# A decoder layer on one core: scaling, casts, sums and weights in a new order between w_o and the second SwiGLU, and in the first pair of both SwiGLUs

## The reference, cut to what matters

```
x = x + 1/2 * gate1(c) * SwiGLU_1(adaLN_1(RMSNorm(x), c))
h = adaLN_2(RMSNorm(x), c)
y = W_o( sigmoid(g_nsa(h)) * Up_nsa(NSA(h)) + sigmoid(g_fox(h)) * Up_fox(FoX(h)) )
x = x + gate2(c) * y
x = x + 1/2 * gate3(c) * SwiGLU_2(adaLN_3(RMSNorm(x), c))
out = RMSNorm(x)

rms_norm(x, g)  = x * rsqrt(mean(x * x) + eps) * g
swiglu(h)       = (silu(h @ w_gate) * (h @ w_up)) @ w_down        # 1024 -> 2816 -> 1024
```

## Time and profile before

| | us |
|---|---|
| median of 3 runs | 2421.49 |
| lowest and highest | 2418.65, 2422.41 |
| the profiled execution, device time | 2420.48 |
| its span, first to last instruction | 2418.8 |
| mean granted TensorE clock in it | 0.985 |

### The profile page before, as it was taken

How to read it: one execution, slowest core, us unless ns; L and a number is a source line. 1 busy time by engine, 2 the same in 40 slices (tenths; PEclk the granted TensorE clock), 3 DMA queues, 4 the chain that set the end, 5 groups by cost and what they waited for, 6 DMA issues and landing times. The chain is left out here.

```text
span 2418.8 us, 30082 instructions
## 1 busy us (share of the span) xinstructions
PE 2310.0 (96%) x10920; PEld 1881.7 (78%) x10920; DVE 1394.3 (58%) x1667; ACT 1087.5 (45%) x2060; POOL 1251.1 (52%) x964
## 2 busy tenths in 40 slices
PE   4999999999999899999999999999989999999997
PEld 2788888888878777778777877787768888888885
DVE  5845565356556755653688888568663323325544
ACT  3533333333444543334788888424533333323332
POOL 3454444444664555445557555456645555535463
PEclk7999999999999999999999999999999999999998
DMA  6145544265442433443814046324212222245362
GB/s 251 66 183 183 187 178 153 74 230 169 148 158 79 122 123 110 154 165 126 240 40 115 18 101 161 120 88 148 96 66 75 104 70 88 79 174 170 118 193 85
DMA packets 128946, 314.98 MB, mean 130 GB/s; under 512 B 13408, under 2 KB 34016, under 8 KB 128800
## 3 DMA queue, kind: packets, MB, share of 16 engines
q1 hardware_dynamic: 127824, 310.76, 38.5%
q10 hardware_dynamic: 976, 2.29, 0.4%
HBM read 241.51 MB, written 69.34 MB: 129 GB/s over the span
## 5 line engine op out<-in xcount | busy, mean ns | idle before, releaser
L1667 POOL TENSOR_TENSOR r_z<-f_main,r_z 128x512 fp32r<-128x512 f32 x254 | 354.8, 1399 | 386.3 <-ACT r_z L1057 386.3
L2598 PE MATMUL ps<-r_main,r_z 128*128 128x512 f32 x1232 | 484.2, 393 | 18.8 <-issue 10.8
L2599 PE MATMUL ps<-r_main,r_z 128*128 128x512 f32 x1232 | 482.4, 392 | 0.0
L2600 PE MATMUL ps<-r_main,r_z 128*128 128x512 f32 x1232 | 482.3, 392 | 0.0
L1673 POOL TENSOR_TENSOR r_main<-f_main,r_main 128x1024 fp32r<-128x1024 f32 x88 | 218.9, 2491 | 218.1 <-ACT r_main L1098 218.1
L2598 PEld LDWEIGHTS ps<-r_main,r_z 128*128 128x128 f32 x1232 | 233.2, 189 | 69.1 <-issue 16.6
L2574 PE MATMUL ps<-r_main 128*128 128x512 f32 x688 | 268.9, 391 | 2.6 <-DVE r_main L2044 2.6
L2600 PEld LDWEIGHTS ps<-r_main,r_z 128*128 128x128 f32 x1232 | 233.0, 189 | 49.1
L2599 PEld LDWEIGHTS ps<-r_main,r_z 128*128 128x128 f32 x1232 | 233.2, 189 | 48.6 <-issue 0.2
L2576 PE MATMUL ps<-r_main 128*128 128x512 f32 x688 | 267.8, 389 | 0.0
L2575 PE MATMUL ps<-r_main 128*128 128x512 f32 x688 | 267.7, 389 | 0.0
(11 more groups left out here) (325 smaller groups left out, 4624.1 us busy)
## 6 DMA issues: line engine op xcount, KB each, us to landing
f_main<-in_wd SPq DMA_DIRECT2D x88, 512.0 KB, 3.6
f_main<-in_w_ada SPq DMA_DIRECT2D x56, 512.0 KB, 5.0
act_d<-f_main SPq DMA_DIRECT2D x88, 256.0 KB, 2.0
f_main<-act_d SPq DMA_DIRECT2D x88, 256.0 KB, 3.7
f_main<-in_wg SPq DMA_DIRECT2D x20, 1024.0 KB, 5.0
f_main<-in_wu SPq DMA_DIRECT2D x20, 1024.0 KB, 4.9
f_main<-in_wmix SPq DMA_DIRECT2D x18, 1024.0 KB, 5.1
r_main<-qk_hi_d SPq DMA_DIRECT2D x40, 256.0 KB, 7.4
```

Of the source, the lines that this page charges most:

```text
L1667: pool.tensor_tensor(prod_lo_t[slot], source_of(g), prod_hi_t[slot].bitcast(F32), ALU.subtract).then_inc(s["wl"], 1)
L2598: pe.matmul(out, wh, hi, start=start, stop=False, skip_group_check=True)
L2599: pe.matmul(out, wh, lo, start=False, stop=False, skip_group_check=True)
L2600: return pe.matmul(out, wl, hi, start=False, stop=stop, skip_group_check=True)
```

## The change: what it does

Nothing is computed that was not computed before, apart from one sum that goes from POOL to DVE. What changes is the place of instructions in the lists of ACT, DVE and POOL, and where one intermediate lies:

- **w_o:** `piece22(1)` on DVE stands ahead of the steps 6 and later, no longer inside step 9.
- **Sums of squares:** square 13 is added on DVE, into `sum_p[1]`, no longer on POOL; POOL adds square 5 after its last weight low of w_o. `stat(2, 1)` stands after the second tile of x, no longer after the first.
- **Into the second SwiGLU:** ACT does tile 0's shift and cast ahead of squares 15 and 12, then tile 1, square 14, tiles 2 and 3, tile 4, and then the root for half 1. POOL scales tiles 2 to 5 in one go, then lows 4 and 5, tile 6, lows 6 and 7, tiles 7 to 15.
- **First pair of both SwiGLUs:** x is cast in the order q = 7, 6, 5, 4; T1 and T3 follow each low of q 3; weight sums 3 and 1 of pair 1's gate come before q 7's lows, sum 2 in the middle of them. The take of g = 10 (u3) and sums 3 and 1 of pair 1's up half stand inside `first_pair`; ACT's takes of g = 8 and 9 too. `plain_taken` 2 and 3 come last. Sum 2 of pair 1's up half goes to step 13 (from step 10).
- **p7 of pair 1's gate** is kept in `x[:, 4, half 1]`, a tile of x that is used up by then, and no longer in `act_q[3]`, whose store had to be waited for; that wait goes to the Silu after q 5.

The core of the diff:

```diff
+X_ORDERS = [(1, 2, 8, 3, 7, 6, 5, 4), X_ORDER, (1, 2, 8, 3, 7, 6, 5, 4)]
+FIRST_SUMS = [(1, GATE, n) for n in (3, 1, 2, 4)] + [(1, UP, n) for n in (3, 1)]
-        for n, early in ((3, 7), (1, 7), (2, 5), (4, 2)):
-            if (p, b) != (1, GATE):
+        for n, early in ((3, 7), (1, 7), (2, 2 if p == 1 else 5), (4, 2)):
+            if (p, b, n) not in FIRST_SUMS:
...
-O_SUM_P = [1, 2, 3, 5, 13]
-O_SUM_D = [9, 10, 11, 6, 7, 12, 14]
+O_SUM_P = [1, 2, 3, 5]
+O_SUM_D = [9, 10, 11, 6, 7, 13, 12, 14]
...
+        def p7_of_pair(p, b):
+            return p7_up if b == UP else x[:, 4, halves(1)] if p == 1 else act_q[3]
...  ACT, taken
                 elif q == 7:
-                    if p > 0:
+                    if p > 1:
                         act.wait_ge(s["st"][3], z["st"] + 16 * p)
-                    act.copy(act_q[3], bank_e[b]).then_inc(s["p7"], 1)
+                    act.copy(p7_of_pair(p, b), bank_e[b]).then_inc(s["p7"], 1)
                 elif q == 5:
                     act.wait_ge(s["c22"], z["c22"] + u + 1)
+                    if p == 1:
+                        act.wait_ge(s["st"][3], z["st"] + 16 * p)
-                    act.activation(act_q[3], act_q[3], ACT.Silu).then_inc(s["sil"], 1)
+                    act.activation(act_q[3], p7_of_pair(p, b), ACT.Silu).then_inc(s["sil"], 1)
...  ACT, first_pair
-                for m in range(4, 16):
-                    if m + 1 < 16:
-                        shifted(k, m + 1)
+                for m in range(4 + k // 2, 16):
+                    if k == 2 or m + 1 < 16:
+                        shifted(k, m if k == 2 else m + 1)
                     x_high(k, X_ORDER[m // 4], m % 4)
...
                 weight_high(f, 9)
+                for i in range(2):
+                    x_high(k, 6, i)
+                weight_high(f, 10)
+                weight_high(f, 11)
+                for i in range(2, 4):
+                    x_high(k, 6, i)
                 for i in range(4):
-                    x_high(k, 6, i)
-                for g in (10, 11, 12):
-                    weight_high(f, g)
-                plain_taken(f, 2)
+                    x_high(k, 5, i)
+                taken(f, 8)
                 for i in range(4):
                     x_high(k, 4, i)
+                taken(f, 9)
+                weight_high(f, 12)
                 weight_high(f, 13)
+                weight_high(f, 14)
+                plain_taken(f, 2)
                 plain_taken(f, 3)
-                taken(f, 8)
-                for i in range(4):
-                    x_high(k, 5, i)
-                weight_high(f, 14)
...  ACT, from w_o into the second SwiGLU
             for g in range(4):
                 weight_high(1, g)
+            shifted(2, 0)
+            act.wait_ge(osem["mm"], O_LATE)
+            x_high(2, 1, 0)
             out_square(15)
-            shifted(2, 0)
             out_square(12)
             shifted(2, 1)
-            act.wait_ge(osem["mm"], O_LATE)
-            x_high(2, 1, 0)
-            shifted(2, 2)
             x_high(2, 1, 1)
             out_square(14)
             for m in range(2, 4):
-                shifted(2, m + 1)
+                shifted(2, m)
                 x_high(2, 1, m)
+            shifted(2, 4)
+            x_high(2, 2, 0)
             std(2, 1)
...  DVE, first_pair (new text)
                for i in range(4):
                    x_low(k, 3, i)
                    t1_t3(k, i)
                weight_sum(f, 1, GATE, 3)
                weight_sum(f, 1, GATE, 1)
                for i in range(4):
                    x_low(k, 7, i)
                    t2(k, i)
                    if i == 1:
                        weight_sum(f, 1, GATE, 2)
                plain_taken(f, 0)
                plain_taken(f, 1)
                (x_low q 6, t4, weight_sum GATE 4, x_low q 5)
                taken(f, 10)
                weight_sum(f, 1, UP, 3)
                (x_low q 4)
                weight_sum(f, 1, UP, 1)
                plain_taken(f, 2)
                plain_taken(f, 3)
...  DVE, w_o
                 elif q == 5:
-                    if u > 0:
+                    if u > 1:
                         piece22(u)
...
             piece22(0)
             for i in range(4):
                 out_x_low(3, i)
+            piece22(1)
...  DVE, from w_o into the second SwiGLU
             x_low(2, 1, 0)
+            out_taken(27)
+            out_square_sum(13)
             out_square_sum(12)
-            out_taken(27)
             x_low(2, 1, 1)
             out_square_sum(14)
             for i in range(2, 4):
                 x_low(2, 1, i)
+            x_low(2, 2, 0)
             reciprocal(2, 1)
...  PE
-                            if k == 2 and (h, part, i) == (0, 0, 0):
+                            if k == 2 and (h, part, i) == (0, 0, 1):
                                 stat(2, 1)
```

More of the change, by code:

```diff
@@ L1633, in out_square_sum @@
             def out_square_sum(j):
-                s, h, before = nsem, j // NT, O_SUM_P.index(j)
+                s, before = nsem, O_SUM_P.index(j)
                 pool.wait_ge(s["sq"], SQ[2] + O_SQ.index(j) + 1)
-                if j == 13:
-                    pool.wait_ge(s["sd"], SUM_D[2] + O_SUM_D.index(11) + 1)
-                elif before > 0:
+                if before > 0:
                     pool.wait_ge(s["sp"], SUM_P[2] + before)
                 square = sq_f[O_SQ.index(j) % 3]
-                pool.tensor_tensor(sum_p[h], sq_f[O_SQ.index(0) % 3] if j == 1 else sum_p[h], square, ALU.add).then_inc(s["sp"], 1)
+                pool.tensor_tensor(sum_p[0], sq_f[O_SQ.index(0) % 3] if j == 1 else sum_p[0], square, ALU.add).then_inc(s["sp"], 1)
             def scaled(k, m, u=None):
@@ L1863, in out_square_sum @@
                 dve.wait_ge(s["sq"], SQ[2] + max(O_SQ.index(j), O_SQ.index({9: 8, 6: 4, 12: 15}.get(j, j))) + 1)
-                total, square = sum_p[1] if j in (9, 10, 11) else sum_d, sq_f[O_SQ.index(j) % 3]
+                total, square = sum_p[1] if j in (9, 10, 11, 13) else sum_d, sq_f[O_SQ.index(j) % 3]
                 if j in (9, 6, 12):
@@ L1996, in first_pair @@
             def first_pair(f, k):
-                for q in (2, 8, 3):
-                    for i in range(4):
+                for q in (2, 8):
+                    for i in range(1 if (k, q) == (2, 2) else 0, 4):
                         x_low(k, q, i)
                 for i in range(4):
+                    x_low(k, 3, i)
                     t1_t3(k, i)
+                weight_sum(f, 1, GATE, 3)
+                weight_sum(f, 1, GATE, 1)
                 for i in range(4):
```

63 lines of the change are left out of this document (33 added, 30 removed).

## The result

| | before | after |
|---|---|---|
| median of 5 runs, us | 2421.0 | 2410.73 |
| lowest and highest | 2418.65, 2422.41 | 2406.97, 2411.18 |
| the profiled execution, its span | 2420.48, 2418.8 | 2406.97, 2405.2 |
| mean granted TensorE clock in it | 0.985 | 0.988 |

The ratio of after to before is 0.9955, with a 95% interval from 0.9941 to 0.997. So the change makes the kernel 10.3 us faster (0.45%), where 21 us were forecast, and 2410.73 lies above the range of 2396 to 2406. The profiled execution is the fastest of its five; four of them are 1.3 to 4.2 us slower.

The account below looks back on a forecast made before the run. PE was taken to bound both stretches the change touches. The terms 1.9 + 1.5 + 4.8 + 13.3 = 21.5 us, against the profiled 2420.48, gave 2399.0, as a median 2400.0, with a range of 2396 to 2406.

Parts of the forecast that it names:

- u3 in the first SwiGLU: First SwiGLU, wait at g = 12: u3 would follow g = 10 at once; gain 1.9 us, bounds 0 and 1.9.
- at nothing: Parts priced at no cost: p7 in a tile of x, square 13 on DVE, plain_taken 2 and 3 last.
- piece22(1) in w_o: w_o: the 1.8 us wait goes, 0.3 kept for POOL; gain 1.5 us, bounds 0.5 and 1.8.
- Handover: From w_o into the second SwiGLU: 3.5 + 1.7 - 0.5 + 0.1 = 4.8 us gained; bounds 2 and 6.
- the half clock of 1.7: Handover, behind tile 0: with only a 1.0 us wait left, the 1.7 us lost at half clock go too.
- Tile 0: Handover, second SwiGLU's first tile: PE starts at 1710.4, 3.5 of 4.5 us gained, a 1.0 us wait left.
- Tile 1: Handover, second tile: wanted at 1713.1, ready between 1712.7 and 1715; a new wait of 0.5 us.
- the handover stays slow in another form: Rival, chance 0.09: several short waits, DVE and POOL colliding, clock perhaps falling again; 5 us lost, 2405.
- Pair 1: Second SwiGLU: waits at g = 10 and g = 12 go with their half clock; 13.3 us, or 6 if one returns.
- a wait comes back in pair 1: Rival, chance 0.13: slow DVE rows make u3 late in the second SwiGLU; 7.5 us lost, 2407.5.
- The change doesn't do what it says: Rival, chance 0.03: PE meets the same releasers, lists only shuffled; within 4.8 us of before.
- Slower: Rival, chance 0.03: sum 2 of pair 1's up half at step 13 delays ACT's step 11; 2422 to 2426.

Follow-up runs that it names:

- narrow weight lows: Changed kernel with POOL's weight lows of g = 12 to 16 in both SwiGLUs cut to 8 columns; 2402.84 us, ratio 0.9932.
- the cast held: Changed kernel with ACT's cast of the g = 15 weights held until q 4's lows are done: 2405.72 us; with c22 also moved ahead, 2406.09.
- c22 first alone: Changed kernel with c22 (DVE's take of g = 12) right behind q 4's lows, ahead of sum 1 and plain_taken 2 and 3; 2410.91 us, ratio 0.9962.
- the old handover: Changed kernel with the sums' tables and ACT's, POOL's and DVE's order from w_o to the last scaling put back; 2412.1 us, ratio 0.997.
- `piece22(1)` alone: Kernel before the change with only piece22(1) of w_o moved ahead of DVE's steps 6 and later; 2418.95 us beside 2418.57, ratio 0.9998.
- second profile: Changed kernel run and profiled once more, with nothing altered; median 2410.91 us, ratio 0.9963.

## Why the prediction was wrong

**u3 in the first SwiGLU: 1.9 forecast, 0.1 measured.** The wait at g = 12 went, as said; u3 was there in time. PE gave it all back at g = 14, where it waits 1.37 us. The step that failed is the one "at nothing": `plain_taken` 2 and 3 last, ahead of products ten steps on. I asked who wants them, and not who stands behind them: c22, wanted two products on. It was on time only if the lows before it took 0.69. That is the deeper part of the step: with the lows of q 4 unslowed (narrow weight lows, or the cast held) the first SwiGLU keeps its 1.9 us although c22's place is the same, and with c22 first alone the gain is lost again at the up half.

**piece22(1) in w_o: 1.5 forecast; 1.8 at its place, nothing in the median by itself.** The mechanism at its place was right. The 0.3 that I kept for POOL did not appear. What I did not ask is what the clock does behind it; by the mean clocks it is the likely taker, in a stretch that no profile here shows.

**Handover: 4.8 forecast; 2.2 in the profiled execution (5.2 less 3.0), 0.6 where the half clock comes back, 1.7 by the median with the old handover (1.2 or 2.8 by its trace).** My times stood on the clock of before, so 3.0 us of lead are to be added to those of after. Tile 0 gave 3.0 of 3.5: PE started it at 1710.7 on that clock (1710.4 forecast) after a wait of 1.21 (1.0 forecast). Weight low 7 stayed, at 0.72 (0.9 forecast), and small pieces took 0.3. Two sizes were wrong. Tile 1 cost 2.0 in place of 0.5. Its cast was done at 1711.4 (1711.3 forecast), but DVE came to its low only at 1713.8, where I had 1712.0 to 1713.5, and took 1.75 us for it, where I had 0.7 to 1.6: the two sums ahead of it took 1.11 and 1.78, since POOL's scalings of tiles 2 to 5 run beside them. So it was late by more than my worst case, 1715, and DVE waited for itself, not for ACT. And the half clock of 1.7 went only once in six profiles. My reason was that single waits of up to 1.72 us left the clock high. Here 1.2 and 1.9 us stand within 5 us. And the reason was weak even for single waits, as a place far from the change shows: in every kernel PE waits 1.8 us near 915, alone. In seven of the 13 profiles the clock stays up behind it, in the other six it falls. PE there, in the kernel before and in the one with `piece22(1)` alone:

```profile
915.31 0.47 PE L2767 MATMUL ps<-r_main,r_z 128*128 128x512 f32 x1 [1.81 <-DVE ps L2186]
```

```profile
916.89 0.55 PE L2768 MATMUL ps<-r_main,r_z 128*128 128x512 f32 x1 [1.82 <-DVE ps L2186]
917.24 0.63 PE L2769 MATMUL ps<-r_main,r_z 128*128 128x512 f32 x1
```

So one execution with a high clock behind such a wait, which is all that the earlier trace rows had, says little.

This is the rival "the handover stays slow in another form", to which I gave 0.09. The Trainium skill (TensorE: Matmul & The Clock Gate, "A second HAM failure mode: psum-queue depth-cycling") had spoken for it; the windows with 0.94 behind two such waits, and with 1.00 where the second is 0.2, agree with that rule in kind.

**Pair 1: 13.3 forecast, 8.3 measured.** Both long waits and their half clock went, 12.4 up to g = 13, nearly as worked out; 0.7 is left at g = 12. There DVE's margin of 2 us was gone (u3 ended at 1767.79, forecast 1766.1), and weight low 12, forecast for 1765, ended at 1768.3, since its cast stood behind the casts of q 4. (PE itself was ready for g = 12 at 1767.66, forecast 1768.0, so the two clocks agree there.) But then "a wait comes back in pair 1", the rival with 0.13, in small pieces, of which 4.2 us lie between the second tile of g = 13 and g = 14. That rival's stated price, 7.5, was for a clock that falls too; it didn't. The step that failed: the working ends at u3. The lows of q 4 and c22 behind it, which PE wants next, stand in no term. The cause is also in my reason against the rival, "POOL has only four lows in that stretch". POOL had five, in one go, from just ahead of u3 on and beside the one group of DVE's instructions that PE is waiting for. The average of DVE's rows was not the question; which ones collide was. The Trainium skill (SBUF — State Buffer, "Who interferes with whom") says that DVE with two SBUF inputs and POOL wait for each other's whole instruction; I had used this rule for one tile and not for the run of four lows. The trace agrees for the wide lows: 6.85 us for four lows beside 7.50 for four of POOL's, and 2.49 where POOL's are narrow; while u3, which reads one operand from PSUM, takes 0.69 at 1767.10 and 0.70 at 112.45 with POOL busy beside it.

**The other rivals.** "The change doesn't do what it says" is out. "Slower", sum 2 of the up half at step 13, does not decide, but its mechanism exists: with the cast of g = 15 held, ACT waits for that sum and the seed copy behind it comes 1.3 us late.

**The sum.** In the profiled executions 0.1 + 1.2 (from the first SwiGLU to w_o, nothing of the change, largely the clock) + 1.8 + 2.2 + 8.3 = 13.6, against 13.5 measured. The median is 3.2 less than that. A half clock behind tile 1 explains 1.7. More of it is likely the half clock that comes and goes behind two single waits far from the change, 1.8 us near 915 and 2.0 near 956, which all 13 profiles have. Eight of them show it behind one of the two, the profile of before among them, and the first two of the changed kernel behind neither; that is also where the 1.2 us before w_o come from. That no edit decides it is argued from the waits, which are the same in all kernels, and not shown.

**The signs.** I had called the forecast wrong "if a wait of over 2 us stands in pair 1, or if the clock drops behind the handover". In the first profile neither was so. The signs missed a row of waits of 0.3 to 1.5 us, and the clock fell only in the second profile. Two slips of the working changed nothing: g = 10 ends one product before 114.9 and not two (the 112.1 is right), and the best case as a median, 2421.5 - 23 - 1.5, is 2397 and not 2396.

## What to carry to other kernels

When a list of instructions is reordered so that one engine is early, price its work by what the other engine will be streaming at that moment in the new order, not by an average of the old trace; a burst of POOL may land on the very instructions that are awaited. Ask of an instruction put "last" also who stands behind it. Follow the engine's list past the wait that is being removed, to the next instructions that are wanted. Do not book a half clock as won while waits of a microsecond or two remain, and take the profile of more than one execution before reading a gain of less than 1%.

## What the runs showed of the hardware

- DVE's and POOL's instructions on two SBUF operands of 128x512 alternate one by one when both have a queue of them: 1.7 us for one of each, where each alone takes 0.6 and some 1.3. Both lose. A DVE instruction that reads one operand from PSUM is not slowed (u3, 0.69 and 0.70, with POOL's lows beside it).
- POOL's lows of 128x8 are shown with up to 3.00 us beside DVE's lows and 0.20 alone, though lengths on POOL are rough. DVE's four took 2.49 then: POOL was held up and DVE was not, where with wide lows both were.
- The same program with the same waits (within 0.03 us) had a granted clock of 1.00 in one execution and 0.94 in the next, over 30 us behind waits of 1.2 and 1.9 us.
- Behind a single wait of 1.8 us near 915 the granted clock from 913 to 923 is 1.00 in seven profiles and 0.83 in six; behind one of 2.0 near 956 it is 1.00 from 954 to 962 in eleven and 0.79 in two. What decides stays open.
